# Two wide gate projections by seven half-size products, ahead of the branch projections, with the branch inputs kept in DRAM meanwhile

## The reference, cut to what matters

```python
h = rmsnorm(x, norm_mix_g)                     # 512 x 2048
u = h @ w_in                                   # 2048 x 12288, ten splits
c_g, b_g, xa, za, q, fl, iv, og, ga, gb = split(u)   # ga, gb: 2048 wide, the others 1024
ya = b_g * causal_dwconv3(c_g * xa) * silu(za)
yb = norm(hgrn2(q, fl, iv)) * silu(og)
m = sigmoid(ga) * (ya @ w_a_out) + sigmoid(gb) * (yb @ w_b_out)
x = x + m @ w_o
```

## Time and profile before

| | |
|---|---|
| median of three runs | 2509.98 us (2509.73 to 2510.24) |
| span of the profiled execution, first to last instruction | 2508.7 us |
| PE busy | 2502.2 us, 12614 matmuls |
| DVE busy | 1358.9 us |
| ACT busy | 918.4 us |
| POOL busy | 149.5 us |
| granted TensorE clock | 1.000 |
| ga0 starts at, wb3 ends at (from the span's start) | 742.15 us, 1264.39 us |

### The profile page before, as it was taken

One profiled execution on the slowest core, in us unless ns is written; L12 is line 12 of the kernel. 1 busy time (PEld: TensorE's weight loads), 2 busy tenths in 40 slices (PEclk: granted clock), 3 DMA queues, 4 the chain that ended last, 5 costly groups with the idle time before them and its releaser, 6 DMA issues.

```text
span 2508.7 us, 31305 instructions
## 1 busy us (share of the span) xinstructions
PE 2502.2 (100%) x12614; PEld 2075.9 (83%) x12614; DVE 1358.9 (54%) x2248; ACT 918.4 (37%) x1259; POOL 149.5 (6%) x195
## 2 busy tenths in 40 slices
...
GB/s 192 110 96 95 96 105 95 95 95 100 100 93 164 213 218 214 218 212 212 149 161 110 93 101 93 93 101 178 92 76 76 85 125 101 113 106 112 178 101 101
DMA packets 213633, 317.95 MB, mean 127 GB/s; under 512 B 66736, under 2 KB 69680, under 8 KB 212464
## 3 DMA queue, kind: packets, MB, share of 16 engines
...
## 4 chain that ended last, share of the span: by engine, by line
PE 100%; ACT 0%; DVE 0%; issue 0%; ACTq 0%; DVEq 0%
PE bank L366 94%; PE bank L1449 1%; PE bank L1450 1%; PE bank L1451 1%; PE bank L798 0%; PE bank L857 0%; PE bank L782 0%; PE bank L860 0%; PE bank L825 0%; PE bank L1841 0%; PE bank L1955 0%; PE bank L1953 0%; PE bank L1954 0%; PE bank L467 0%; ACT OT L2266 0%; PE bank L472 0%
## 5 line engine op out<-in xcount | busy, mean ns | idle before, releaser
L366 PE MATMUL bank<-XH,WH 128*128 128x512 f32 (+1 forms) x2776 | 1078.7, 390 | 0.0
L366 PE MATMUL bank<-XH,WL 128*128 128x512 f32 (+1 forms) x2776 | 1074.5, 389 | 0.0
L366 PE MATMUL bank<-XL,WH 128*128 128x512 f32 (+1 forms) x2776 | 1074.0, 389 | 0.0
L418 DVE TENSOR_TENSOR WL<-RAW,WH 128x1024 fp32r<-128x1024 f32 x430 | 530.1, 1234 | 760.6 <-ACT WH L395 760.0
L395 ACT CAST WH<-RAW 128x1024 fp32r<-128x1024 f32 x430 | 450.1, 1048 | 1113.4 <-PE bank L366 1102.2
L366 PEld LDWEIGHTS bank<-XH,WL 128*128 128x128 f32 x2776 | 521.0, 188 | 108.1 <-DVE WL L418 0.2
L366 PEld LDWEIGHTS bank<-XH,WH 128*128 128x128 f32 x2776 | 521.0, 188 | 107.7 <-ACT WH L395 0.2
L366 PEld LDWEIGHTS bank<-XL,WH 128*128 128x128 f32 x2776 | 521.2, 188 | 107.1 <-issue 0.5
L366 PE MATMUL bank<-WH,XL 128*128 128x512 f32 x384 | 149.4, 389 | 0.0
L366 PE MATMUL bank<-WH,XH 128*128 128x512 f32 x384 | 149.4, 389 | 0.0
L366 PE MATMUL bank<-WL,XH 128*128 128x512 f32 x384 | 149.4, 389 | 0.0
...
## 6 DMA issues: line engine op xcount, KB each, us to landing
RAW<-in_w_in SPq DMA_DIRECT2D x303, 512.0 KB, 3.8
AST<-in_w_ada SPq DMA_DIRECT2D x192, 256.0 KB, 4.1
RAW<-in_w_o SPq DMA_DIRECT2D x32, 512.0 KB, 3.7
RAW<-in_w_gate SPq DMA_DIRECT2D x32, 512.0 KB, 3.6
RAW<-in_w_out SPq DMA_DIRECT2D x32, 512.0 KB, 3.7
RAW<-in_w_a SPq DMA_DIRECT2D x16, 512.0 KB, 4.2
RAW<-in_w_b SPq DMA_DIRECT2D x16, 512.0 KB, 4.3
PT<-ZT SPq DMA_DIRECT2D x256, 32.0 KB, 1.9
```

Source lines behind the costliest of these rows:

```text
L366: ins = nc.tensor.matmul(bank[b][:, cols], l, r[:, cols], start=first, stop=final)
L418: nc.vector.tensor_tensor(low_of(m), RAW[:, m % NRAW], high_of(m).bitcast(F32), ALU.subtract).then_inc(lo.sem, lo.step(m))
```

## The change

1. The order becomes ga0 to ga3, gb0 to gb3, wa0 to wa3, wb0 to wb3, wo.
2. A group of ga or gb is computed as a 2 x 2 block product (input features in two halves of 1024, tokens in two halves of 256, output columns in two halves of 256) by seven half products in place of eight. Each unit takes one block of 128 features from each half. A product is 128 x 256 weights times 128 x 256 tokens: two blocks of output columns, three matmuls each, of **256** columns. A unit is then 42 matmuls of 256 columns, where it was 24 of 512. The seven products of a group lie in seven banks.
3. The four sums of weights that this takes are made for every unit by POOL (`weight_sums_pool`, four instructions of 128 x 256 with two SBUF inputs). ACT casts, and DVE subtracts, in two instructions for a unit: 768 elements of plain weights and 1024 of sums.
4. The four sums of tokens are made during og1 for each of eight pairs of blocks: DVE adds the high and low parts (1024 elements), POOL makes four sums, ACT casts in two instructions, DVE subtracts in two (768 and 256 elements).
5. After a group of seven products ACT copies the first, DVE does eight additions from PSUM into `OUT7`, ACT does two sigmoids of 1024 elements, and issues a DMA of 1 MB to DRAM. Before, ACT did four sigmoids of 512 from PSUM.
6. SBUF is needed: `ya` (2 MB) and the heads (2 MB) are stored to DRAM in og0/og1 and at the start of ga0, and read back during gb3 and wa; the gates are read back in pieces of 1 MB during wa and wb.
7. "ada": 96 of the 192 row blocks in ga and gb, with two buffers, the others from wa0 on, with three; a pace of 0.9 a step throughout. Its last sums (`modulation_dve`) stand ahead of `proj`.
8. Splits: `ya` at the end of gb3 and in wa0, the heads into `XH`, `XL` during wa1, `m` during wb3.

The core of the diff:

```diff
+    for name, w, nk, c in (("ga", "w_in", 16, ga), ("gb", "w_in", 16, gb), ("wa", "w_a", 8, 0), ("wb", "w_b", 8, 0)):
+        for g in range(4):
+            add((name, g), w, 0, nk, c + 512 * g)
...
+SEVEN = range(FIRST["ga", 0], FIRST["wa", 0])
+PRODUCTS = ("11", "12", "s2", "s3", "s1", "s4", "22")
+ADA_EARLY, ADA_PACE = 96, 0.9
...
     def split_free(m):
+        if m in SEVEN:
+            n = m - SEVEN[0]
+            if n == 1:
+                return [(dense, ("unit", SEVEN[0] - 1))]
+            if n < 3:
+                return [(xlo, ("t2", 7)), (dve, ("silu", ("og", 1), 3))] if n else [(xlo, ("t2", 7))]
+            return [(dense, ("unit", m - 3))]
...
+                if m in SEVEN:
+                    u = (m - SEVEN[0]) % 3
+                    nc.scalar.copy(WH7[u][:, 0:3], raw_blocks(m)[:, 0:3]).then_inc(hi.sem, hi.step(("plain", m)))
+                    A.wait_ge(pool, (yield pool, ("s4", m)))
+                    nc.scalar.copy(WH7[u][:, 3:7], SUMS[m % 2][:, :, :]).then_inc(hi.sem, hi.step(m))
+                    continue
...
+    def seven_pe(name):
+        mine = take(7, 0, 8)
...
+        for u in range(8):
...
+            for i, which in enumerate(PRODUCTS):
...
+                for j in range(2):
...
+                    nc.tensor.matmul(b, left_high, right_high, start=u == 0 and j == 0, stop=False, skip_group_check=True)
+                    nc.tensor.matmul(b, left_high, right_low, start=False, stop=False, skip_group_check=True)
+                    ins = nc.tensor.matmul(b, left_low, right_high, start=False, stop=u == 7, skip_group_check=True)
...
+    def token_sums_dve():
...
+        for u in range(10):
+            if u > 1:
+                k = u - 2
+                V.wait_ge(xhi, (yield xhi, ("t", k)))
+                nc.vector.tensor_tensor(TXL[:, :, k], HF[k % 2][:, 0:3], TXH[:, :, k].bitcast(F32), ALU.subtract
+                                        ).then_inc(xlo.sem, xlo.step(("t", k)))
+                V.wait_ge(xhi, (yield xhi, ("t2", k)))
+                nc.vector.tensor_tensor(XL[:, k, SECOND_HALF], HF[k % 2][:, 3], XH[:, k, SECOND_HALF].bitcast(F32),
+                                        ALU.subtract).then_inc(xlo.sem, xlo.step(("t2", k)))
+            if u < 8:
...
+                nc.vector.tensor_tensor(HF[u % 2][:, :, :].rearrange("p (a b) c -> p a (b c)", a=2),
+                                        XH[:, u:u + 9:8].bitcast(F32), XL[:, u:u + 9:8].bitcast(F32), ALU.add
+                                        ).then_inc(dve.sem, dve.step(("rows", u)))
+            yield
...
+    def weight_sums_pool():
+        for m in SEVEN:
...
+            G.wait_ge(raw[m % NRAW], (yield raw[m % NRAW], m))
+            if m - SEVEN[0] > 1:
+                G.wait_ge(lo, (yield lo, m - 2))
+            elif m % 2:
+                G.wait_ge(dense, (yield dense, ("unit", SEVEN[0] - 1)))
+            nc.gpsimd.tensor_tensor(s1, a21, a22, ALU.add).then_inc(pool.sem, pool.step(("s1", m)))
+            nc.gpsimd.tensor_tensor(s3, a11, a21, ALU.subtract).then_inc(pool.sem, pool.step(("s3", m)))
...
+            nc.gpsimd.tensor_tensor(s2, s1, a11, ALU.subtract).then_inc(pool.sem, pool.step(("s2", m)))
...
+            nc.gpsimd.tensor_tensor(s4, a12, s2, ALU.subtract).then_inc(pool.sem, pool.step(("s4", m)))
...
+        def reload_ya():
+            for k in range(4):
+                yield from idle(3)
+                Y.wait_ge(dense, (yield dense, ("unit", FIRST["gb", 3] + 2 * k + 1)))
+                nc.sync.dma_start(YA[:, k:k + 5:4], ya_dram[:, k:k + 5:4]).then_inc(ld[f"ya{k}"].sem, ld[f"ya{k}"].step(0))
+                yield
```

More of the change, by code:

```diff
@@ new lines, in seven_out_act @@
+    def seven_out_act(name):
+        out, n = OUT7[gate_index(name) % 2], gate_index(name)
+        A.wait_ge(dense, (yield dense, (name, 0)))
+        if n < 2:
+            A.wait_ge(o_spilled, (yield o_spilled, 0))
+        else:
+            A.wait_ge(gates_spilled[n % 2], (yield gates_spilled[n % 2], n - 2))
+        nc.scalar.copy(quarter(out, 0, 0), bank[banks[name][0]][:, :].rearrange("p (j t) -> p j t", j=2)
+                       ).then_inc(ev_a.sem, ev_a.step((name, 0)))
+        for half, last in enumerate(("s4", "s1")):
+            A.wait_ge(ev_d, (yield ev_d, (name, PRODUCTS.index(last))))
+            A.use(SIG)
+            nc.scalar.activation(out[:, 2 * half:2 * half + 2], out[:, 2 * half:2 * half + 2], ACT.Sigmoid
+                                 ).then_inc(act.sem, act.step(("gate", n, half)))
+        A.wait_ge(act, (yield act, ("gate", n, 1)))
+        nc.scalar.dma_start(gates_dram[:, 4 * n:4 * n + 4], out[:, :, :]
+                            ).then_inc(gates_spilled[n % 2].sem, gates_spilled[n % 2].step(n))
@@ new lines, in token_sums_act @@
+    def token_sums_act():
+        A.wait_ge(dve, (yield dve, ("o", 7)))
+        yield
+        for k in range(8):
+            A.wait_ge(pool, (yield pool, ("t2", k)))
+            A.wait_ge(pool, (yield pool, ("t4", k)))
+            nc.scalar.copy(TXH[:, :, k], HF[k % 2][:, 0:3]).then_inc(xhi.sem, xhi.step(("t", k)))
+            A.wait_ge(dense, (yield dense, ("unit", FIRST["og", 1] + k // 2)))
+            nc.scalar.copy(XH[:, k, SECOND_HALF], HF[k % 2][:, 3]).then_inc(xhi.sem, xhi.step(("t2", k)))
+            yield
@@ L1209, in c_act, with ada_act @@
         A.use(SIG)
-        nc.scalar.activation(SGT[:, :], CB[:, q % 2], ACT.Sigmoid).then_inc(act.sem, act.step(("c", q)))
-    def ada_act():
-        yield from c_act(0)
+        nc.scalar.activation(SGT[:, :], c_row(q), ACT.Sigmoid).then_inc(act.sem, act.step(("c", q)))
+    def ada_act(first, last):
+        yield from c_act(first // 48)
         yield
-        for n in range(192):
-            q, t = divmod(n, 48)
-            if t == 24 and q < 3:
-                yield from c_act(q + 1)
+        for n in range(first, last):
+            if n == 48:
+                yield from c_act(1)
+            if n == 120:
+                yield from c_act(3)
             yield
@@ L2046, in act_program @@
[L2046 to L2065 removed]
+        ya_feed = Feed(split_act("ya", YH, YA, YA_MADE))
@@ new lines, in act_program @@
+        turns.specials.append(ada_act(0, ADA_EARLY))
+        turns.pace = ADA_PACE
+        for name in ("ga", "gb"):
+            for g in range(4):
+                if name == "gb" and g == 3:
+                    turns.chores.append(idle(7))
+                    turns.chores.append(rows_of(ya_feed, 2))
+                yield from act_dense((name, g))
+                yield from seven_out_act((name, g))
+        yield from turns.finish(turns.specials)
+        turns.specials.append(ada_act(ADA_EARLY, 192))
@@ L2485, in dve_program @@
                                         ).then_inc(ev_d.sem, ev_d.step((("wo", g), i)))
+        yield from turns.finish(turns.specials)
+        turns.pace = 1.0
+        yield from modulation_dve()
         for g in range(4):
@@ L2656, in sp, with spill_ya, spill_heads @@
                 yield from sp_dense((name, half))
+        def spill_ya():
+            yield from idle(4)
+            Y.wait_ge(dve, (yield dve, ("silu", ("za", 1), 3)))
+            nc.sync.dma_start(ya_dram, YA[:, :, :]).then_inc(ya_spilled.sem, ya_spilled.step(0))
+            yield
+        def spill_heads():
+            yield from idle(2)
+            Y.wait_ge(dve, (yield dve, ("silu", ("og", 1), 3)))
+            nc.sync.dma_start(o_dram, O[:, :, :]).then_inc(o_spilled.sem, o_spilled.step(0))
+            yield
+        turns.chores.append(spill_ya())
         yield from sp_dense(("og", 0))
@@ new lines, in reload_rest @@
+        def reload_rest():
+            yield
+            Y.wait_ge(xlo, (yield xlo, ("ya", 3)))
+            load_gate(ld["sga0"], 0, M[:, 0:4], 0)
+            yield
+            for n in (6, 7):
+                Y.wait_ge(gates_spilled[n % 2], (yield gates_spilled[n % 2], n))
+            nc.sync.dma_start(O[:, :, :], o_dram).then_inc(ld["o"].sem, ld["o"].step(0))
+            yield from idle(4)
+            Y.wait_ge(xlo, (yield xlo, ("ya", 7)))
+            for g in range(1, 4):
+                load_gate(ld[f"sga{g}"], 0, M[:, 4 * g:4 * g + 4], g)
+                yield from idle(4)
+            load_gate(ld["sgb"], 0, SG[:, :, :], 4)
+            yield
```

323 lines of the change are left out of this document (223 added, 100 removed), and 2 rows, old and new, of the table ld.

## The result

The changed kernel takes 2556.64 us (median of four runs, 2556.53 to 2556.93) against 2510.11 beside it: a ratio of 1.0185, 95% interval 1.0171 to 1.02, so **46.5 us slower**. The prediction was 2525.7 with a range from 2489 to 2554, so the result lies 2.6 us above the range. The span of the profiled execution is 2555.3 us (2508.7 before).

The account below looks back on a forecast made before the run. PE alone bounds the kernel before; DVE and POOL excluding each other would delay it after. Groups +1.7 (PE's saving included), og1 +9, entry +4, rest +1 make +15.7 on span 2508.7: 2524.4, median 2525.7 us, range 2489 to 2554.

Parts of the forecast that it names:

- PE's own work, 322.6 us: ga and gb: 2688 matmuls of 256 columns at 120.0 ns each, 25.6 us less than before.
- Rival 3: ga and gb: weight loads set a short matmul's price, 188 ns, +157 us, 2667 us; chance 0.03.
- ada's product takes part: ga and gb: ada's DVE instruction also excludes POOL, 14.4 pieces x 0.55 = 7.9 us a group.
- Rival 1: ga and gb: PE stays the bound, ada's instruction not excluding POOL or instructions falling well; 2493 us, chance 0.22.
- ada's DMAs, 1.6 us a group: ga and gb: 1.6 us a group added for landings of ada's DMAs with two buffers.
- og1, +9: og1: token sums exclude 5.0 us a pair against PE's 2.72 a step; PE waits 9 us, bounds 0 to 14.
- the sum: Whole kernel: the prediction's terms added, 1.7 + 9 + 4 + 1 = +15.7 us, span 2524.4.
- Entry into ga0, +4: Start of ga0: unit 2's weights come late behind DVE's silu, 13.3 us against 10.1; 4 us, 0 to 8.
- rival 2: ga and gb: ada's DMA waits block DVE, or waits lower PE's clock; 48 to 50 a group, 2545 to 2562; chance 0.17.
- group term, 44.4 and 40.3: ga and gb: 6.7 groups with ada at 44.4 us, 1.3 without at 40.3; 349.9 us, 1.7 more than before.
- Rival 1's partial case: ga and gb: 42 us a group, with 14 for the rest: -6 us, 2504; raises faster's chance from 0.22 to 0.27.
- the signs that I had named: Profile after: 120 ns matmuls, og1 idle some 9 us, longer POOL and DVE means, groups 43 to 46, gb2 and gb3 40.3.

Follow-up runs that it names:

- run 1: Changed kernel with POOL's four weight sums per unit replaced by four fills of 768 elements that read nothing: 2519.42 us.
- run 2: Changed kernel with ada's early product on 16 of 512 columns, all DMAs and waits kept: 2529.15 us.
- run 8: Kernel before the change, with each 512-column matmul of ga and gb made as two of 256: 2530.5 us.
- Run 6: Changed kernel with token sums begun in og0, og1's silu ahead of unit 1's casts and subtractions, ada five pieces later, last two products swapped: 2541.02 us.
- Run 12: Run 10 with ACT copying product 11 first at group ends, sigmoids and store moved into the next group, ada's pace 0.6 in wb3, 1.45 in wo1-wo3: 2497.05 us.
- run 9: Run 7 with DVE's eight additions at a group's end put ahead of the subtractions for the next group's second unit: 2521.93 us, ratio 1.0044.
- run 10: Run 9 with other paces of ada behind gb3, from 0.3 in wo0 to 1.35: 2521.22 us, ratio 1.0045.
- run 7: Run 6 with 48 of ada's pieces early at pace 0.45, later 1.2 in wa, 1.3 in wb, 0.5 in wo0, 1.25 in wo: 2526.43 us.
- run 11: Run 9 with 96 of ada's pieces early at pace 0.85 and the rest at 0.9, 0.4 in wo0: 2538.45 us, ratio 1.0112.

## Why the prediction was right, and where it was wrong

**Right: the direction and its reason.** I forecast slower, since DVE and POOL would exclude each other while PE had the smaller work. Runs 1 and 2 show it. Of the terms below, PE's work, ada's part and ada's DMAs came out by their own reasons; og1 and the entry are near in size, and only in part for the reason given.
- *PE's own work, 322.6 us.* Measured 119.97 ns a matmul undisturbed, 120.05 in run 8. Rival 3 (188 ns) is out. The Trainium skill (TensorE: Matmul & The Clock Gate, Back-to-back issue gap) gives a gap for an isolated matmul that makes 109 ns at 256 columns, an estimate by its rule; these matmuls take 11 ns more.
- *ada's product takes part.* 1050 ns beside POOL's sums, 689 beside fills. Rival 1 is out.
- *ada's DMAs, 1.6 us a group.* DVE's idle time before ASTE is 10.5 us over some 6.7 groups.
- *og1, +9.* Waits of 9.3, on low parts, as forecast, but from the fifth of og1's units on (722), where the sum had the seventh late (731). And the group grew by 13.5, since the low clock has no term.
- *Entry into ga0, +4.* Partly luck. The term was a wait for the weights of unit 2, late behind silu. PE's first wait, 4.18 us up to 763.57, comes earlier and is for a bank of og1 that silu frees, which the prediction didn't look at; one of 2.8 us for a low part follows at 783. Run 6 took ga0 from 55.01 to 41.60 with silu ahead and ada later, so more than the 4 hung on this entry.

**Wrong: the size, 30.9 us short in the span (2555.3 against 2524.4).** The step that failed is the sum, which priced a wait at its own length. The low clock that follows a wait stood only in rival 2, at chance 0.17, and has no term in the sum: it measured **15.6 us in ga and gb and 4.0 in og1** by the distances, about three fifths of the miss (14.8 of the 15.6 and 3.7 of the 4.0 beside a clock of 0.5). Rival 2's price, 2545 to 2562, held the result; its second reason was the true one (the clock), its first (ada's DMAs) wasn't, as DVE waited for them as little as I had reckoned.

The second failed step is the **group term, 44.4 and 40.3**. It counted amounts, as if a full DVE were enough to know and all delays could be evened out. The waits in ga and gb were 38.6 us where the sum implied 31.3 (27.3, and 4 for the entry): 7.3 more. What failed is less the size than the path: the term had groups stretched evenly, and 27 us of the waits stand behind the groups' ends, since the additions were late in DVE's order: 3.69 us at 1048.91, 2.4 to 3.7 at most others. Run 12 shows this: with ada's pace in these groups as in runs 9 and 10, another order of the same work takes the sum from 346.0 to 325.0. Run 9 alone took 2.2 off run 7's 348.2. Even gb2 and gb3, for which I took 40.3, measured 45.75 and 44.10 with ada running only to 1081.8, in the last of them not at all. Amounts matter beside it (run 11, 29 us for 48 pieces). I take the two not to be separate terms: in run 12 a good order did with little slack, DVE at 34.1 and POOL at 37.4 of 40.33 us. With ada's amount as in the changed kernel that order wasn't run.

The rest is small: wo +2.3, wa0 +0.3 and the ends +1.9 where I had 1 for all.

One sum of the prediction is wrong in itself. Rival 1's partial case takes 6.7 x -2.4 from 44.4 us, but 1.3 x -3.2 from the 43.52 of the kernel before; from 43.52 throughout, 42 us a group gives 6.7 x -1.5 - 4.2 + 14, about 0, so 2510 and not 2504. So the 0.27 for faster stood on too much. The prediction also has rows 5 agree with a lock for the whole length of an instruction; they show 1.14 of 1.30 and 1.09 of 1.22 us, as its own sum uses.

Among the signs that I had named, POOL's and DVE's longer means and the 120 ns came; the groups didn't: 43 to 46 us were named and 44.6 to 52.9 measured, and gb3, without ada, took 44.10, not 40.3. A clock under 1.00 in a window wasn't on the list, and should have been.
